# Retention in a block of transformer layers: values before the pairs, output projections one head behind

## The reference

```python
q, k, v, g = jnp.split(a @ w_in, [hk, 2 * hk, 2 * hk + hv], axis=-1)   # hk = 4*256, hv = 4*512
q, k = apply_rope(q, *rope), apply_rope(k, *rope)                      # latent tokens only
k = k * RET_DK ** -0.5
# per head: o[t] = sum over s of decay(t, s) * (q[t] . k[s]) * v[s], in both directions of time,
# the context first; decay(t, s) = gamma_h ** |t - s|
y = rms_norm_2(o)                                                      # over the 512 features of a head
return (jax.nn.silu(g) * y) @ w_out
h_lat = layer_norm(alpha * h_lat + m * y_lat, ...)
```

## Time and profile before

| | us |
|---|---|
| median of 3 runs | 2769.79 |
| lowest, highest | 2769.33, 2770.24 |
| the profiled execution | 2770.4 |
| its span, first to last instruction | 2768.6 |
| TensorE busy | 2733.4 |
| VectorE busy | 2013.9 |
| ScalarE busy | 1290.1 |
| granted TensorE clock, mean | 0.999 |

### The profile page before, as it was taken

One profiled execution on the slowest core, in us unless ns is written; L12 is line 12 of the kernel. 1 busy time (PEld: TensorE's weight loads), 2 busy tenths in 40 slices (PEclk: granted clock), 3 DMA queues, 4 the chain that ended last, 5 costly groups with the idle time before them and its releaser, 6 DMA issues.

```text
span 2768.6 us, 42922 instructions
## 1 busy us (share of the span) xinstructions
PE 2733.4 (99%) x16374; PEld 2452.4 (89%) x16374; DVE 2013.9 (73%) x3722; ACT 1290.1 (47%) x2380; POOL 372.8 (13%) x207
## 2 busy tenths in 40 slices
PE   9999999999999999999999999999999999999998
PEld 8888896988888899988888999999997787989898
DVE  7788778868896888865555996667685536778686
ACT  6332358642333645553243744344355546545354
POOL 2343300022433000011101000000002323000000
PEclk9999999999999999999999999999999999999999
DMA  6655512236654154333322022222223121222322
GB/s 204 193 186 190 168 64 84 77 110 210 191 189 152 52 206 153 126 129 141 128 75 78 25 64 74 77 65 65 76 77 96 50 81 51 75 85 92 107 92 84
DMA packets 98206, 307.48 MB, mean 111 GB/s; under 512 B 10192, under 2 KB 25424, under 8 KB 96464
## 3 DMA queue, kind: packets, MB, share of 16 engines
q1 hardware_dynamic: 90368, 279.42, 31.3%
q10 hardware_dynamic: 7632, 25.30, 2.3%
HBM read 282.53 MB, written 20.58 MB: 109 GB/s over the span
## 4 chain that ended last, share of the span: by engine, by line
PE 60%; DVE 6%; issue 2%; DMA 1%; ACT 1%; POOL 1%; ACTq 0%; DVEq 0%; SPq 0%; POOLq 0%
PE ps L2232 19%; PE ps L2233 18%; PE ps L2234 18%; DVE t_wlo L2977 1%; PE ps L2515 1%; PE ps L2499 1%; PE ps L2488 1%; DMA t_raw<-in_gu 1%; ACT t_whi L2558 1%; DVE t_m L3228 0%; POOL t_wlo L3677 0%; DVE t_mw L3075 0%; DVE t_m L3050 0%; DVE t_hid L3563 0%; DVE t_m L3297 0%
## 5 line engine op out<-in xcount | busy, mean ns | idle before, releaser
L2558 ACT CAST t_whi<-t_raw 128x512 fp32r<-128x512 f32 (+3 forms) x494 | 381.5, 783 | 592.2 <-PE ps L2234 391.6
L2232 PE MATMUL ps<-t_h,t_whi 128*128 128x256 f32 (+2 forms) x1852 | 624.1, 337 | 7.1 <-DVE t_wlo L2968 1.9
L2233 PE MATMUL ps<-t_h,t_wlo 128*128 128x256 f32 (+2 forms) x1852 | 619.4, 334 | 0.0
L2234 PE MATMUL ps<-t_h,t_whi 128*128 128x256 f32 (+2 forms) x1852 | 619.3, 334 | 0.0
L2977 DVE TENSOR_TENSOR t_wlo<-t_raw,t_whi 128x512 fp32r<-128x512 f32 (+3 forms) x420 | 355.3, 857 | 105.1 <-ACT t_whi L2558 101.3
L2232 PEld LDWEIGHTS ps<-t_h,t_whi 128*128 128x128 f32 x1852 | 350.3, 189 | 41.8 <-issue 10.6
L2233 PEld LDWEIGHTS ps<-t_h,t_wlo 128*128 128x128 f32 x1852 | 350.5, 189 | 26.4 <-issue 0.5
L2234 PEld LDWEIGHTS ps<-t_h,t_whi 128*128 128x128 f32 x1852 | 350.4, 189 | 26.0
L2232 PE MATMUL ps<-t_hid,t_whi 128*128 128x256 f32 (+2 forms) x1032 | 335.5, 325 | 0.6 <-DVE t_hid L3276 0.6
L2233 PE MATMUL ps<-t_hid,t_wlo 128*128 128x256 f32 (+2 forms) x1032 | 333.6, 323 | 0.0
L2234 PE MATMUL ps<-t_hid,t_whi 128*128 128x256 f32 (+2 forms) x1032 | 333.1, 323 | 0.0
(11 more groups left out here) (375 smaller groups left out, 4939.6 us busy)
## 6 DMA issues: line engine op xcount, KB each, us to landing
t_raw<-in_gu SPq DMA_DIRECT2D x174, 512.0 KB, 3.4
t_raw<-in_ada SPq DMA_DIRECT2D x96, 512.0 KB, 3.8
t_raw<-in_dn SPq DMA_DIRECT2D x52, 512.0 KB, 4.1
t_raw<-in_dn SPq DMA_DIRECT2D x24, 384.0 KB, 3.4
s_qk<-t_hid ACTq DMA_DIRECT2D x12, 768.0 KB, 5.7
t_hid<-s_qk SPq DMA_DIRECT2D x6, 1536.0 KB, 11.4
t_raw<-in_ret_v SPq DMA_DIRECT2D x16, 512.0 KB, 5.2
t_raw<-in_ret_g SPq DMA_DIRECT2D x16, 512.0 KB, 3.8
```

Of the source, the lines that this page charges most:

```text
L2232: e.matmul(out, whi, xlo, start=first, stop=False, skip_group_check=shared)
L2233: e.matmul(out, wlo, xhi, start=False, stop=False, skip_group_check=shared)
L2234: return e.matmul(out, whi, xhi, start=False, stop=last, skip_group_check=shared)
L2558: e.copy(m.block(0, it.slot, n), m.raw(it)).then_inc(*S["hi"].of(j))
```

## The change

Only retention is changed.

- The values of all four heads are made before the first pair, two token tiles at a time. Each tile (hi and lo, 1024 columns) is stored to HBM from a ring of 8 places in HID and comes back per head, tile by tile, into H, once the tile of the head before has been used.
- `early_gate` and `late_gate` are gone; gates 2 and 3 of head 3 are a pair of seven products. Query/key and gate pairs alternate throughout.
- The output projection of head h-1 follows `attend(h)`; the last two follow each other. Gates, outputs and gated values have two sets of places, by h % 2; head 1's queries and keys get a place of their own in H.
- The context key tiles come first in a head (order 4, 5, 0, 1, 2, 3).
- The decay table is loaded and made in two parts: 640 columns (`short_table`) in the middle of the head before, 896 columns (`long_table`) at its end.
- `qk_load` and `g_load` move from SyncE's to ScalarE's queue.
- `from_bank(4)` before the output projection is gone; it stays before value products.

```diff
@@ keys and values
-        keys = {512: (4, 5), 0: (0, 1, 2, 3, 4, 5)}
+        keys = {512: (4, 5), 0: (4, 5, 0, 1, 2, 3)}
         def v_rows(h):
             from_bank(4)
-            rows([("ret_v", h, blk) for blk in range(4)], 4, ov["v"], ("ret_v", h), lambda tt: RVV + tt * 512, pairs=h == 0,
-                 low_dest=lambda tt: (4096 if h == 0 else RVL) + tt * 512, aside=h == 0)
+            ring = lambda tt: (h * 6 + (4, 5, 0, 1, 2, 3).index(tt)) % 8
+            rows([("ret_v", h, blk) for blk in range(4)], 4, lambda tt: [(f"d_vs{ring(tt)}", ov["ring"][ring(tt)])] if ring(tt) in ov["ring"] else state["hid_free"],
+                 ("ret_v", h), lambda tt: ring(tt) * 1024, pairs=True, low_dest=lambda tt: ring(tt) * 1024 + 512,
+                 done=lambda g: v_store(h, g.tt, ring(g.tt)))
@@ the tables
+        def long_table(h, free_rest, turned):
+            put("dist_load", h=h, part=0, after=free_rest)
+            put("ret_decay", h=h, after=turned)
+        def short_table(h, free_sides, after):
+            put("dist_load", h=h, part=1, after=free_sides)
+            put("side_decay", h=h, after=after)
@@ def attend(h)
                 if (t0, i) == (0, 1):
                     finish(h, 512, 256)
-                    gated_values(h, 512, 256, range(4 if h < n_head - 1 else 3))
-            if h == n_head - 1:
-                from_bank(4)
-                late_gate(h, 3, ov["oc"])
-                gated_values(h, 512, 256, (3,))
+                    gated_values(h, 512, 256)
+                    if h < n_head - 1:
+                        short_table(h + 1, [("drain_dve", ("ret_p", h, 0, 1))], [e for k in range(4) for e in slots.get(("b", k), [])])
+                        free([("b", k) for k in range(4)], ("ret_gs", h + 1))
+            if h < n_head - 1:
+                long_table(h + 1, [("drain_dve", ("ret_p", h, 0, 5))], [("p_lo", (h, 0, 5))])
             finish(h, 0, 512)
@@ the order
-        early_gate(n_head - 1, 2)
+        for h in range(1, n_head):
+            v_rows(h)
         wide_slots(384)
...
-            if k != 3:
-                last = seven_pair("g", *gate_pairs[k - (k > 3)])
+            last = seven_pair("g", h, w)
         back_to_slots(384)
+        tokens_read, sums_read = [("ps", last["P2"])], [("ps", last["P4"])]
+        values_back(0, lambda tt: tokens_read)
+        put("qk_load", h=1, after=tokens_read + [*kept[1]])
+        for h in range(2):
+            put("g_load", h=h, after=sums_read + stores[h])
         for h in range(n_head):
             attend(h)
             if h < n_head - 1:
-                put("dist_load", h=h + 1, after=[("drain_dve", ("ret_p", h, 0, 5))])
-                put("ret_decay", h=h + 1, after=[("p_lo", (h, 0, 5))])
-            if h < n_head - 1:
-                v_rows(h + 1)
-                put("qk_load", h=h + 1, after=[("ret_ps", ("s", h, 0, 5))] + [staged[w] for w in range(2)])
+                values_back(h + 1, lambda tt, h=h: [("ret_ps", ("v", h, 0, keys[0].index(tt), 3))])
+                if h != 1:
+                    put("qk_load", h=max(h + 1, 2), after=[("ret_ps", ("s", h, 0, 5)), *kept[max(h + 1, 2)]])
...
-            if h < n_head - 1:
-                from_bank(4)
-            done = columns([(("ret_o", j2, h), (2, 512), 4, ("yr", h), outs(j2)) for j2 in range(4)],
-                           SUB2 if h == 3 else SEG2, batch=4 if h == 3 else 1)
-            if h < n_head - 1:
-                put("g_load", h=h + 1, after=[done] + stores[h + 1])
+            if h:
+                done = output(h - 1)
+                if h + 1 < n_head:
+                    put("g_load", h=h + 1, after=[done] + stores[h + 1])
+        ov["oc"] = [output(n_head - 1)]
@@ TensorE's part
     def ret_value(it):
         w.wait_ge("p_lo", (it.h, it.t0, it.i))
-        if it.h:
-            w.wait_ge("drain_dve", (("ret_v", it.h), it.kt))
-        else:
-            w.wait_ge("d_rv0" if it.kt >= 4 else "d_rv1", 0)
+        w.wait_ge(f"d_rv{it.kt}", it.h)
@@ ScalarE's part
+    def side_decay(it):
+        h, gs, tb = it.h, m.at(RST + 896, 640), m.side_sum(it.h)
+        w.wait_ge("d_dist1", h)
+        w.wait_ge("ret_dve", "nlb")
+        wait_all(it.after)
+        e.activation(tb, gs, ACT.Exp, scale=m.sm(4 + h, 1), bias=m.sm(20 + h, 1)).then_inc(*S["ret_act"].of(("g2", h)))
         w.wait_ge("ret_act", ("g2", h))
         e.activation(gs, gs, ACT.Exp, scale=m.sm(8 + h, 1)).then_inc(*S["ret_act"].of(("g1", h)))
+    def v_store(it):
+        w.wait_ge("drain_act", (("ret_v", it.h), it.tt))
+        w.wait_ge("drain_dve", (("ret_v", it.h), it.tt))
+        e.dma_start(dram["s_v"][it.h][:, it.tt * 1024:it.tt * 1024 + 1024], m.HID[:, it.at * 1024:it.at * 1024 + 1024].bitcast(F32)).then_inc(
+            *S[f"d_vs{it.at}"].of((it.h, it.tt)))
@@ VectorE's part
     def ret_score(it):
         w.wait_ge("ret_ps", ("s", it.h, it.t0, it.i))
-        w.wait_ge("ret_ll", it.h)
-        w.wait_ge("ret_gs", it.h)
+        if it.t0 == 0 and it.kt >= 4:
+            w.wait_ge("ret_dve", ("d3", it.h))
+            w.wait_ge("ret_gs", it.h)
+        else:
+            w.wait_ge("ret_ll", it.h)
```

More of the change, by code:

```diff
@@ L692, in rows, with rows_by_group @@
             pass
-    def rows_by_group(srcs, ver, after, key, dest, order=(4, 5, 0, 1, 2, 3), pairs=False, banks=(), early=0, low_dest=None, aside=False):
+    def rows_by_group(srcs, ver, after, key, dest, order=(4, 5, 0, 1, 2, 3), pairs=False, banks=(), early=0, low_dest=None, done=None):
         held = [block(s, (SLOT,)) for s in srcs]
@@ L719, in rows_by_group @@
             for g in late:
-                put("rows_split" if low_dest else "rows_copy", g=g.id, bank=g.bank, after=after, key=(key, g.tt), dst=dest(g.tt),
-                    low=low_dest and low_dest(g.tt), aside=aside)
+                put("rows_split" if low_dest else "rows_copy", g=g.id, bank=g.bank, after=after(g.tt) if done else after, key=(key, g.tt), dst=dest(g.tt),
+                    low=low_dest and low_dest(g.tt))
+                if done:
+                    done(g)
             late = []
@@ L1519, in finish, with gated_values, output, values_back @@
             put("ret_recip", h=h, t0=t0, n=n)
-        def gated_values(h, t0, n, some):
-            for c in some:
+        def gated_values(h, t0, n):
+            for c in range(4):
                 put("ret_y", h=h, c=c, t0=t0, n=n)
                 put("ret_split", h=h, c=c, t0=t0, n=n)
-        ov["v"] = state["hid_free"]
+        def output(h):
+            chain = lambda s: layer_norm_chain(
+                s, "l00", 0, lambda c, s: [("drain_dve", ("l00", 3, c, s))], after_ln("l00", 5, 0, 0, 3), True)
+            post = gated("l00", 0, 2, 3, chain, lambda j, s: [("x_alpha", (j, s))])
+            outs = lambda j2: [(jj * 512, "drain_dve", lambda g, j=j2 * 2 + jj, h=h: post(h, j, g)) for jj in range(2)]
+            return columns([(("ret_o", j2, h), (2, 512), 4, ("yr", h), outs(j2)) for j2 in range(4)],
+                           SUB2 if h == 3 else SEG2, batch=4 if h == 3 else 1)
+        def values_back(h, after):
+            for tt in keys[0]:
+                at = (h * 6 + (4, 5, 0, 1, 2, 3).index(tt)) % 8
+                put("v_load", h=h, tt=tt, at=at, after=after(tt))
+        ov["ring"] = {}
+        pro = state["misc_free"] + [("ps", ("root", "nf2", s)) for s in range(2)] + [("ada", (1, 47, who)) for who in range(2)]
         v_rows(0)
-        put("v_store")
-        pro = state["misc_free"] + [("ps", ("root", "nf2", s)) for s in range(2)] + [("ada", (1, 47, who)) for who in range(2)]
         put("ret_setup", after=pro)
@@ L1534, in retention @@
         sides[:] = [pro] * 4
-        early_gate(n_head - 1, 2)
+        for h in range(1, n_head):
+            v_rows(h)
         wide_slots(384)
-        ov["qk"] = [[("d_vs0", 0)], [("d_vs0", 0)]]
+        ov["qk"] = [[(f"d_vs{at}", ov["ring"][at]) for at in range(8)]] * 2
         state["quad"] = [("gate_pool", ("f2", "rs", s)) for s in range(2)]
-        gate_pairs = [(1, 0), (1, 1), (2, 0), (2, 1), (3, 0), (0, 0), (0, 1)]
         pairs = [(h, w) for h in (1, 2, 3, 0) for w in range(2)]
-        for k, (h, w) in enumerate(pairs):
+        for h, w in pairs:
@@ L1549, in retention @@
+            last = seven_pair("g", h, w)
+            kept[h] = list(staged.values())
         back_to_slots(384)
-        last_h = [("ps", last["P4"])]
-        put("v_load", after=[("ps", last["P6"])])
-        put("g_load", h=0, after=last_h + stores[0])
-        ov.update(oc=last_h, p=[rope_done, rope_done, last_h], v=[])
+        tokens_read, sums_read = [("ps", last["P2"])], [("ps", last["P4"])]
+        values_back(0, lambda tt: tokens_read)
+        put("qk_load", h=1, after=tokens_read + [*kept[1]])
@@ L2445, in ret_score @@
             if it.h:
-                w.wait_ge("d_qk", it.h)
+                w.wait_ge(f"d_qk{it.h}", "all")
             else:
@@ L2845, in qk_store @@
                 *S[f"d_qs{it.w}"].of((it.h, part), it.h))
```

(5 more changed lines are left out.)

187 lines of the change are left out of this document (79 added, 108 removed).

## The result

The changed kernel takes 2787.74 us (median; runs from 2784.29 to 2789.25) beside 2769.79 us for the kernel before on the same chip: a ratio of 1.0064, 95% interval 1.005 to 1.0079. It is 18 us slower, where I had forecast 8 us faster. The time lies outside the range that I gave (2757.8 to 2770.8).

The account below looks back on a forecast made before the run. TensorE was taken as the bound, with waits at retention's start, after adjacent query/key pairs, at heads 1 to 3, and in the last output projection. From 2770.4 us, 10.7 off, 2.8 on, 0.6 off gave 2761.9, range 2757.8 to 2770.8.

Parts of the forecast that it names:

- Parts 1 and 2: Sixteenth pair as seven products saves 2.1 us; values made before the first pair remove waits of 5.6 and 0.9 us.
- O3 in part 3: Head 3's output projection, moved behind head 2's, loses waits for drained banks and rows of h: 2.1 us off.
- the table of head 1 is wanted at once: Start of head 1: its decay-table exponential would have to run before ScalarE's copies; charged 0.5 us (0 to 4).
- part 4: Reloads issued by ScalarE; head 0's values return after the last product reading the tokens: charged 0.5 us (0 to 2).
- wrong altogether: Sign of failure: TensorE's waits between head 0's scores and its output projection exceed 10 us, or pairs wait for weights.
- casts that come later lose only the issue time: ScalarE's loads wait only for TensorE's earlier step or VectorE, so later casts lose issue time alone; no charge.
- Rival 1: Head 0's squares on ScalarE wait for gate stores behind bulk loads: 5 us above forecast, 2766.9 us; chance 0.40.
- Rival 2: ScalarE also waits for the half table's landing in heads 0 and 1, some 7 us each: 2775.9 us; chance 0.08.
- The half table: Mid-head table switch and two exponentials hold ScalarE about 3 us; charged 0 (0 to 1.5 per head).
- VectorE's crowd in A1: Head 1: VectorE's 32.8 us of work, with head 0's gating, against 30; charged 1.5 us (0 to 4).
- bank 2: Head 1's output projection starts on value bank 2, not bank 4, waiting for its copy; charged 0.3 us (0 to 1.5).
- theory Q: Experiments: ScalarE's queue contents at issue set a small transfer's landing and TensorE's waits; its rival: full DMA engines whatever order.

Follow-up runs that it names:

- e3: Changed kernel, with query/key loads of heads 2 and 3 issued only after VectorE has read the next head's long table: 2772.43 us.
- e1: Changed kernel, with query/key and gate loads issued by SyncE again; values, tables and stores stay on ScalarE: 2776.47 us.
- e6: e5 with each decay table made at one time again, its short part moved to the head's end: 2779.11 us.
- e7: Changed kernel, with only the table loads issued by SyncE: 2770.85 us.
- e2: Changed kernel, with head 1's query/key load issued after head 0's last gate stores have landed: 2781.55 us.
- e4: Changed kernel with the conditions of e2 and e3 together: 2768.44 us.
- e5: e4 with head 1's gate load issued only when head 1's long table has been read: 2765.50 us.
- e8: e5 with the table loads on SyncE's queue too: 2766.32 us.
- e11: e5 with every engine's order frozen, except head 0's gate load moved ahead of head 1's queries and keys: 2765.28 us.
- e12: e11 with head 1's long table also issued ahead of two of head 1's value tiles: 2761.35 us.

## Why the prediction was wrong

**What bounds the kernel** was read rightly: TensorE, and the four places of waits. All of them went.

**Parts 1 and 2, and O3 in part 3: right in place, somewhat small.** I let 10.7 us go. From the account: the printed waits of the kernel before sum to 9.3 us, and in the changed kernel only 1.1 us of waits are left outside the heads (0.8 for ScalarE's L2565 and 0.3 for VectorE's L3008, both in the last pairs); the rest fell by 5.9 us, of which 2.3 is the pair, as computed, and 9 x 0.16 = 1.4 the unprinted part of the waits (15 before, 6 now). Together 8.2 + 5.9 = 14.1 us, where I had 10.7. What the last 2.2 us of the rest are, I can't say.

**Part 3, "the table of head 1 is wanted at once: 0.5 (0 to 4)": the step that failed most.** I saw that the table had lost its cover of 33 us of value products, and priced the order of the exponential and the copies on ScalarE. I never asked when the table lands. The earlier trace rows showed VectorE idle 1.55 us for this load with a quiet queue, and part 4 put 3.1 MB of head 2's queries and keys next to it, both ready at the last score of the head. The cost was 6.0 us before A1 and 5.3 behind A2, with the clock behind each; e3 priced the two together at 15.3 us. My own sign for "wrong altogether", more than 10 us of waits between A0 and O0, came true: 3.2 + 8.9 + 6.0 = 18.1 us.

**Part 4, "casts that come later lose only the issue time": wrong in both halves.** The issue time itself is not small when many follow each other (4.7 us for seven, where a lone one takes 0.33), and it goes with the 3.2 us wait at the start of A0: with six or seven in a row (changed, e1, e3, e6) TensorE waits 2.5 to 3.4 us for these casts, with six and short pauses (e7) 1.3, with four (e2, e4, e5, e8, e11, e12) 1.0 or less. And a small transfer behind a large one is late for whoever waits for it, in whichever program that stands.

**Rival 1 was true, and too small.** Mechanism, place and sign were right (stores at 13.8 to 14.7 us, squares late by 9.62, TensorE by 8.85), and the Trainium skill's rule on ring order, in "DMA: Bandwidth & Descriptors" ("Queues, rings and completion order"), was the reason that I gave it. I took 6 us less 1 of cover; it was 9. I had let 16.8 us pass from the first load to the last landing; from the values' first issue at 1278.77 to the last store's landing at 1302 it was 23. I weighed the rival at 0.40 against 0.45 for my forecast, though no row gave a reason why the planner should put a load of 3.1 MB behind a store that only ScalarE waits for.

**Rival 2 had the right form and the wrong load.** It put two holds of 7 us on the short table. The short table's exponentials did not hold TensorE; the long one's did, before A1 and behind A2. That its price, 14 us, is close to the 15.3 that e3 found for these two is luck: it was worked out for another load. The chance of 0.08 was far too low.

**The rivals were treated as exclusive.** Both come from one cause, bulk loads on the queue of small urgent ones, so they come together: 8.9 + 6.0 + 5.3 + 3.2 = 23.4 us of waits.

**The clock was not in the sum at all.** 8.7 us of the 18. With 14.1 us gained, 24.5 - 1.1 = 23.4 us of new waits and 8.7 us of clock the sum is +18.0, which is the difference of the spans.

**The half table, "I charge 0":** e6 shows that the split is a gain here, of some 6 us. **VectorE's crowd in A1 (1.5) and bank 2 (0.3):** with the loads in order (e12) waits of 2.0 us in A0 and 1.7 in A1 are left, together with shorter ones 5.4, about twice the forecast's 2.8 on top. e12's 2761.35 us lies 0.6 us from my forecast of 2761.9, which was a sum for a kernel whose transfers come in time. In part that is luck: the gains were some 3 us larger than my 10.7 and the waits left over 2.6 us larger than my 2.8.

**What stays open.** Where theory Q missed (e1, e11), the capacity of the DMA engines speaks for the rival: between 1280 and 1310 us the changed kernel has them full in two of three stretches and e5 in all three, and e11 shows that a load brought forward pushes another back. But full engines alone cost TensorE little: in those 30 us of e5 it is busy for 28.3. How much of the remaining 5.4 us is that, and how much VectorE, no run separates. And e7's wide spread goes with its clock, but which waits came and went in its slower runs no profile shows.

## What to carry to other kernels

When a step loses the work that lay between its load and its use, price the load's landing, not only the engines' work: list what is issued ahead of it on its queue, in MB, at the rate that the trace shows for a full queue. A queue on which an engine's small, urgent transfers go (stores whose slots are wanted again, tables, masks) should have no bulk load ahead of them that isn't needed sooner; order by when it is needed, not by when it is ready. And add to a long wait of TensorE the lower clock behind it, here 1.7 us and more each time.

## What the hardware showed

- **The clock behind a wait.** In the changed kernel and in the account's ten versions of it TensorE has 16 waits of 2.5 us and more. Behind, or within, each of them the granted clock fell to 0.50, which cost 1.7 to 3.6 us each; the waits of 24.5 us in the changed kernel cost 8.7 us more that way. Of five waits of 2.0 to 2.5 us two were followed by it (e1's 2.28, e11's 2.22) and three not (e7's 2.29 and 2.49, e12's 1.99).
- **Issues that follow each other closely take longer.** Seven loads from 1278.77 to 1283.46 took ScalarE's sequencer 0.33, 0.42, 0.45, 0.49, 1.13, 0.98 and 0.67 us. How much is still on its way on the queue is not what counts: a store issued alone at 1285.71 and a table load at 1288.22, with head 1's 3.1 MB not yet landed, took 0.33 and 0.34.
- **Two busy queues share by packets, not by bytes.** In e1 they moved 852 and 796 packets in 25 us, but 7.56 and 2.87 MB. Whoever shares with a queue of long packets gets the smaller part.
- **The rate.** From 1290 to 1300 us the changed kernel moved 413 GB/s, e5 401, and e1 10.45 MB in the 25 us from 1300, 418 GB/s: the 411 of the earlier trace rows holds for tens of us, and is what a landing should be priced at.
